# Score matmuls of 64 rows each, squares split for a ones product, more transposes at the start, an earlier merge

## What is computed

```python
u = rmsnorm(h, norm_g[0])
proj = u @ w_in                       # conv parts h, b, c; q, k, v; gates
y_conv = (bc * conv3(cc * hc)) @ w_conv_out
# 4 heads, two maps of 64 channels each, values of 128 channels
s1 = q1 @ k1.T * scale + bias ; s2 = q2 @ k2.T * scale + bias    # bias: -slope * |i - j|
a = softmax(s1) - lam * softmax(s2)
o = rmsnorm(a @ v, subln_g) * (1 - lam_init)
y_attn = o @ w_attn_out
merged = g0 * y_conv + g1 * y_attn    # g: sigmoid(gates + b_gate)
h = h + rmsnorm(merged @ w_o, norm_g[1])
f = square(relu(rmsnorm(h, norm_g[2]) @ w_ff1)) @ w_ff2
out = h + rmsnorm(f, norm_g[3])
```

## Time and profile before

| | us |
|---|---|
| median of 3 runs | 1381.34 (1381.21 to 1382.28) |
| profiled execution | 1382.01 |
| its span | 1380.3 |
| PE busy | 1370.0 (99%) |
| DVE busy | 987.8 (72%) |
| ACT busy | 601.4 (44%) |
| PE without work before the first projection | 1.4, 1.0, 0.8 and 1.0 |

### The profile page before, as it was taken

How to read it: one execution, slowest core, us unless ns; L and a number is a source line. 1 busy time by engine, 2 the same in 40 slices (tenths; PEclk the granted TensorE clock), 3 DMA queues, 4 the chain that set the end, 5 groups by cost and what they waited for, 6 DMA issues and landing times.

```text
span 1380.3 us, 17201 instructions
## 1 busy us (share of the span) xinstructions
PE 1370.0 (99%) x6233; PEld 1119.4 (81%) x6233; DVE 987.8 (72%) x1423; ACT 601.4 (44%) x931; POOL 109.6 (8%) x73
## 2 busy tenths in 40 slices
PE   8999999999999999999999999999999999999998
PEld 7778777778778888888888888888888888888886
DVE  7787796886888754576466887767664787665676
ACT  7544544544543544511243453333333444444453
POOL 0000000000000000000000233333333100000000
PEclk9999999999999999999999999999999999999999
DMA  5111111101101343454721254534445973335343
GB/s 188 46 31 31 31 32 30 45 16 30 46 15 46 108 127 109 135 163 155 270 78 61 88 178 161 167 135 157 158 143 200 364 274 112 99 118 195 112 130 109
DMA packets 141645, 162.02 MB, mean 117 GB/s; under 512 B 6861, under 2 KB 88970, under 8 KB 141450
## 3 DMA queue, kind: packets, MB, share of 16 engines
q1 hardware_dynamic: 135568, 148.27, 33.2%
q10 hardware_dynamic: 6010, 12.88, 2.4%
HBM read 114.98 MB, written 46.14 MB: 117 GB/s over the span
## 4 chain that ended last, share of the span: by engine, by line
PE 97%; DVE 2%; issue 0%; DMA 0%; ACT 0%; DVEq 0%; SPq 0%; ACTq 0%
PE psum L883 37%; PE psum L1004 28%; PE psum L1158 22%; PE psum L1135 3%; PE psum L925 3%; PE psum L970 2%; PE psum L974 1%; PE psum L1107 1%; PE psum L988 0%; DMA xn<-in_x 0%; PE psum L904 0%; DVE z L1829 0%; DVE v L2318 0%; PE psum L913 0%; DVE y L2333 0%
## 5 line engine op out<-in xcount | busy, mean ns | idle before, releaser
L1158 PE MATMUL psum<-op 128*128 128x512 f32 x1344 | 305.1, 389 | 0.1
L1158 PEld LDWEIGHTS psum<-op 128*128 128x128 f32 x1344 | 252.2, 188 | 52.8 <-issue 0.5
L883 PE MATMUL psum<-act_hi,w_hi 128*128 128x512 f32 x448 | 181.9, 406 | 1.0 <-DVE act_lo L1711 1.0
L883 PE MATMUL psum<-act_hi,w_lo 128*128 128x512 f32 x448 | 175.2, 391 | 0.0
L883 PE MATMUL psum<-act_lo,w_hi 128*128 128x512 f32 x448 | 174.5, 390 | 0.0
L2197 DVE TENSOR_TENSOR op<-v,op 128x512 fp32r<-128x512 f32 x112 | 78.6, 701 | 89.3 <-ACT op L1572 89.3
L1572 ACT ACTIVATE op<-v 128x512 fp32r<-128x512 f32 x112 | 70.7, 632 | 151.7 <-PE psum L1158 148.6
L883 PEld LDWEIGHTS psum<-act_hi,w_hi 128*128 128x128 f32 x448 | 84.2, 188 | 21.1 <-issue 4.5
L883 PEld LDWEIGHTS psum<-act_lo,w_hi 128*128 128x128 f32 x448 | 84.3, 188 | 18.0 <-issue 1.9
L883 PEld LDWEIGHTS psum<-act_hi,w_lo 128*128 128x128 f32 x448 | 84.1, 188 | 18.1
L1813 DVE CUSTOM_DVE_ANT_0 e<-psum,alibi 128x1024 f32<-128x1024 f32 x64 | 78.1, 1220 | 6.1 <-issue 5.2
(11 more groups left out here) (267 smaller groups left out, 2803.1 us busy)
## 6 DMA issues: line engine op xcount, KB each, us to landing
f_raw<-f_scratch SPq DMA_DIRECT2D x112, 256.0 KB, 2.7
w_raw<-in_w_in SPq DMA_DIRECT2D x34, 512.0 KB, 4.5
w_raw<-in_w_ff SPq DMA_DIRECT2D x32, 512.0 KB, 5.0
f_scratch<-f_out SPq DMA_DIRECT2D x56, 256.0 KB, 2.4
v<-in_w_ff SPq DMA_DIRECT2D x12, 1024.0 KB, 7.3
gates_scratch<-staging ACTq DMA_DIRECT2D x32, 256.0 KB, 2.0
gate_in<-gates_scratch SPq DMA_DIRECT2D x16, 512.0 KB, 4.2
f_scratch<-staging SPq DMA_DIRECT2D x30, 256.0 KB, 2.1
```

The lines of the kernel that those rows point to most:

```text
L883: mm = nc.tensor.matmul(bank, stat(a, kt), moving(b, kt), start=(n == 0), stop=(n == len(terms) - 1))
L1158: mm = nc.tensor.matmul(psum[:, (X_BANK, Z_BANK)[m % 2][t]], op[n % SLOTS][:, 2 + a, token_cols(t)], op[n % SLOTS][:, b], start=(m in (0, ...
```

## The change

- Score blocks: q and k are no longer stacked. Each is one tile of high parts and one of low parts, both maps one above the other in the 128 rows. For each half of the keys a block runs three passes, and each pass two matmuls of 64 rows, map 0 and map 1. ACT and DVE handle q and k in one instruction of 128 rows per unit.
- `O0` and `O1`: ACT copies the squares as a high part, DVE makes the low part in a new step `L0` or `L1`, and PE runs two `F32R` matmuls with `ones`. PE now waits for the low part. `L0` stands behind `C7` on DVE, `L1` behind `AV1`.
- Start: 34 transposes of the identity before the parameter rows and 6 behind them, instead of 24 and none.
- Gates: for the first gate pair ACT makes one copy out of PSUM earlier; the merge on DVE waits for a tanh two places earlier in their order.

```diff
-DVE_TURN = steps("C7 q0 N0 N1 N2 N3 E0 k0 T7 q1 w0 AV1 k1 w1 N4 ...
+DVE_TURN = steps("C7 L0 q0 N0 N1 N2 N3 E0 k0 T7 q1 w0 AV1 L1 k1 w1 N4 ...
-FROM_LAST_HEAD = steps("C7 O0 N0 N1 N2 N3 E0 T7 AV1 O1 N4 N5 N6 N7 E1")
+FROM_LAST_HEAD = steps("C7 L0 L1 O0 N0 N1 N2 N3 E0 T7 AV1 O1 N4 N5 N6 N7 E1")
-WARM = 24
+WARM = (34, 6)
-        ones = sb("ones", [P, P])
+        ones = sb("ones", [P, P], F32R)
...
+            use_clock(WARM[0])
             pe.wait_ge(par_landed, 16 * 4)
             pe.wait_ge(setup, 3)
             nc.tensor.transpose(psum[:, 7, 0:NPAR], par_rows[:], ident[0:NPAR, 0:NPAR]).then_inc(par_t, 1)
+            use_clock(WARM[1])
...
-                        for c in range(2):
-                            for half in range(NH):
-                                nc.tensor.matmul(psum[:, SB + 2 * c + half], q_st[c][:, n * P:(n + 1) * P],
-                                                 k_st[c][:, half_cols[half]], start=True, stop=False)
                         for half in range(NH):
-                            for c in range(2):
-                                mm = nc.tensor.matmul(psum[:, SB + 2 * c + half], q_st[c][own[c], n * P:(n + 1) * P],
-                                                      k_lo[own[c], half_cols[half]], start=False, stop=True)
+                            for a, b in PASSES:
+                                for c in range(2):
+                                    mm = nc.tensor.matmul(psum[:, SB + 2 * c + half], q_hl[a][own[c], n * P:(n + 1) * P],
+                                                          k_hl[b][own[c], half_cols[half]], start=((a, b) == PASSES[0]),
+                                                          stop=((a, b) == PASSES[-1]))
                         mm.then_inc(s_done, 1)
...
-                        pe.wait_ge(osq_ready, i * 2 + (n - 1))
+                        pe.wait_ge(osq_lo, i * 2 + (n - 1))
                         pe.wait_ge(tb_free, tb_use(i, kind, n))
-                        nc.tensor.matmul(psum[:, TBK], ones[:], dev[:], start=True, stop=True).then_inc(tb_done, 1)
+                        for a in range(2):
+                            mm = nc.tensor.matmul(psum[:, TBK], ones[:], o_sq[n][:, a], start=(a == 0), stop=(a == 1))
+                        mm.then_inc(tb_done, 1)
...
-                            for c in range(2):
-                                for rows in (own[c], other[c]):
-                                    ins = nc.scalar.activation(k_st[c][rows, half_cols[h]], psum[own[c], 1], ACT.Copy)
-                            ins.then_inc(qk_hi, 1)
+                            nc.scalar.activation(k_hl[0][:, half_cols[h]], psum[:, 1], ACT.Copy).then_inc(qk_hi, 1)
...
                         nc.scalar.activation(dev[:], psum[:, TBK], ACT.Square).then_inc(osq_ready, 1)
+                        act.wait_ge(osq_ready, i * 4 - 2 * n + 1)
+                        nc.scalar.activation(o_sq[n][:, 0], dev[:], ACT.Copy).then_inc(osq_ready, 1)
...
                 if p == GATE.first:
                     t_hi_part(GATE, 4)
+                    x_copy(GATE, 2, p)
                 g_part_hi("W11", p + 1)
...
-                if p == GATE.first:
-                    x_copy(GATE, 2, p)
...
+                    elif kind == "L":
+                        dve.wait_ge(osq_ready, i * 4 + 2 * n - 2)
+                        vec.tensor_tensor(o_sq[n][:, 1], dev[:], o_sq[n][:, 0].bitcast(F32), ALU.subtract
+                                          ).then_inc(osq_lo, 1)
...
-            last_turn("C7")
+            last_turn("C7 L0")
...
-            dve.wait_ge(gate_ready, len(GATE_ORDER))
+            dve.wait_ge(gate_ready, GATE_AT[2 * (GATE.end - 1), 0])
```

More of the change, by code:

```diff
@@ L80 @@
                  "T5 X6 M6 b1 T6 X7 M7")
-DVE_TURN = steps("C7 q0 N0 N1 N2 N3 E0 k0 T7 q1 w0 AV1 k1 w1 N4 N5 X0 M0 N6 N7 C0 E1 X1 M1 T0 C1 w2 X2 M2 T1 C2 w3 X3 M3 T2 "
+DVE_TURN = steps("C7 L0 q0 N0 N1 N2 N3 E0 k0 T7 q1 w0 AV1 L1 k1 w1 N4 N5 X0 M0 N6 N7 C0 E1 X1 M1 T0 C1 w2 X2 M2 T1 C2 w3 X3 M3 T2 "
                  "C3 c0 X4 T3 M4 VT0 C4 c1 K0 AV0 X5 w4 M5 T4 C5 b0 X6 M6 T5 C6 X7 b1 w5 M7 T6")
 V_TURN = len([x for x in ACT_TURN[:ACT_TURN.index(("VT", 0))] if x[0] == "T" and x[1] < 7])
-FROM_LAST_HEAD = steps("C7 O0 N0 N1 N2 N3 E0 T7 AV1 O1 N4 N5 N6 N7 E1")
+FROM_LAST_HEAD = steps("C7 L0 L1 O0 N0 N1 N2 N3 E0 T7 AV1 O1 N4 N5 N6 N7 E1")
 TB_ORDER = steps("O0 T7 AV1 O1 T0 T1 T2 T3 VT0 AV0 T4 T5 T6")
@@ L331, in build @@
                 at_hl = [sb(f"at_{a}", [P, TT, HALF], F32R, loop_scope) for a in ("hi", "lo")]
+                with ExitStack() as s1:
+                    o_sq = [None, sb("o_squares1", [P, 2, HALF], F32R, s1)]
                 v_hl = [sb(f"v_{a}", [P, TT, P], F32R, loop_scope) for a in ("hi", "lo")]
@@ L334, in build @@
                 inner = sb("inner", [P, S + 2], scope=loop_scope)
-                q_st = [sb(f"q_stack{c}", [P, S], F32R, loop_scope) for c in range(2)]
-                k_st = [sb(f"k_stack{c}", [P, S], F32R, loop_scope) for c in range(2)]
-                k_lo = sb("k_lo", [P, S], F32R, loop_scope)
+                q_hl = [sb(f"q_{a}", [P, S], F32R, loop_scope) for a in ("hi", "lo")]
+                o_sq[0] = sb("o_squares0", [P, 2, HALF], F32R, loop_scope)
+                k_hl = [sb(f"k_{a}", [P, S], F32R, loop_scope) for a in ("hi", "lo")]
                 with ExitStack() as s1:
@@ L479, in build @@
         zlo_ready = sem("z_lo_ready")
-        osq_ready = sem("o_squares_ready")
+        osq_ready, osq_lo = sem("o_squares_ready"), sem("o_squares_lo_ready")
         orstd_ready = sem("o_inverses_ready")
@@ L540, in build @@
         own = [slice(c * HD, (c + 1) * HD) for c in range(2)]
-        other = [own[1], own[0]]
         half_cols = [slice(h * HALF, (h + 1) * HALF) for h in range(NH)]
@@ L842, in _ @@
                                     pattern=[[-1, P]], channel_multiplier=1).then_inc(setup, 1)
-            nc.gpsimd.memset(ones[:], 1.0).then_inc(setup, 1)
+            nc.gpsimd.memset(ones[:].bitcast(F32), 1.0).then_inc(setup, 1)
             nc.gpsimd.iota(table[:], [[-1, 2 * S - P]], base=S - P, channel_multiplier=1,
@@ L889, in _, with use_clock @@
             pe.wait_ge(setup, 2)
-            for _ in range(WARM):
-                nc.tensor.transpose(psum[:, 6, 0:P], ident[:], ident[:])
+            def use_clock(count):
+                for _ in range(count):
+                    nc.tensor.transpose(psum[:, 6, 0:P], ident[:], ident[:])
+            use_clock(WARM[0])
             pe.wait_ge(par_landed, 16 * 4)
@@ L1261, in walk @@
                         if kind == "q":
-                            for c in range(2):
-                                ins = nc.scalar.activation(q_st[c][own[c], half_cols[h]], psum[own[c], 0], ACT.Copy)
-                            ins.then_inc(qk_hi, 1)
+                            nc.scalar.activation(q_hl[0][:, half_cols[h]], psum[:, 0], ACT.Copy).then_inc(qk_hi, 1)
                         elif kind == "k":
-                            for c in range(2):
-                                for rows in (own[c], other[c]):
-                                    ins = nc.scalar.activation(k_st[c][rows, half_cols[h]], psum[own[c], 1], ACT.Copy)
-                            ins.then_inc(qk_hi, 1)
+                            nc.scalar.activation(k_hl[0][:, half_cols[h]], psum[:, 1], ACT.Copy).then_inc(qk_hi, 1)
                         elif kind == "v":
@@ L1779, in walk @@
                             dve.wait_ge(qk_hi, i * 4 + (2 * h + "qk".index(kind) + 1))
[L1780 to L1784, removed]
+                            hi, lo = (q_hl, k_hl)["qk".index(kind)]
+                            vec.tensor_tensor(lo[:, cols], psum[:, "qk".index(kind)], hi[:, cols].bitcast(F32), ALU.subtract
+                                              ).then_inc(qk_ready, 1)
                         elif kind == "c":
@@ L1979, in _ @@
                 t_sum(GATE, 3, k)
-            last_turn("AV1")
+            last_turn("AV1 L1")
             for k in range(2):
```

2 lines of the change are left out of this document (1 added, 1 removed).

## The result

The changed kernel takes 1392.78 us in the median of four runs (1390.76 to 1396.70), the kernel before 1381.32 (1381.21 to 1382.28). The ratio is 1.0085, with a 95% interval of 1.0061 to 1.0108: slower by 11.5 us. Forecast were 1392.5 us and a range of 1387.2 to 1397.5.

A forecast was written before the change was run, and what follows sets the result against it. PE, busy 1370.0 of 1380.3 us, was taken to bound the kernel. Terms -3.3 + 12.2 - 0.9 + 3.2 = +11.2 us gave 1392.5 us against the median of 1381.34, range 1387.2 to 1397.5.

The forecast's parts named there:

- wait for the low part: PE at `O0` waits for `L0`, queued behind `C7` on DVE, in four places of 2.9 to 3.1 us: +12.2 us.
- ones product: `O0` and `O1` on PE: two `F32R` matmuls replace one float32 product, 0.41 us less, eight times: -3.3 us.
- score blocks: PE's score blocks: six pairs of 64-row matmuls at 0.227 us each take 1.78 us, as before: no change.
- start: Kernel start: more transposes keep the clock at 1.00, first projection moves from 14.59 to 13.73: -0.9 us.
- gates and merge: Gates and DVE's merge: PE has no wait there, and the moved copy and earlier merge change nothing: 0.
- clock behind a stall: PE's clock falls to 0.50 behind two of the four `O0` stalls, 1.6 us each: +3.2 us.
- rival 1: The stalls at `O0` come but the clock never falls: 1389.3 us, chance 0.22.
- What DVE and ACT save on q and k: Fewer copies on ACT and subtractions on DVE per head; PE waits for neither, so worth nothing.
- the pairs' load (3): In the score blocks, pairs in a row keep 0.34 us: 14.6 us more, 1404 to 1407 us, chance 0.07.
- `L0` in time (4): At `O0`, `L0` is done before PE arrives, so no stall: 1377.1 us, faster than before, chance 0.06.

The follow-up runs named there:

- early_l0: The changed kernel with `L0` moved from behind `C7` to between `C6` and `X7` of the same head on DVE: 1378.31 us, ratio 0.9977.
- plain_ones: early_l0 with the ones product again one plain float32 matmul of the squares; copy, subtraction and wait stay: 1381.46 us, ratio 0.9998.
- short_stall: The changed kernel with `L0` one DVE instruction earlier, inside `C7` ahead of its last step: 1385.66 us, ratio 1.0030.
- filled: The changed kernel with 26 identity transposes on PE ahead of each `O0`, the wait for the low part behind them: 1390.68 us, ratio 1.0066.
- early_old_merge: early_l0 with the merge's old wait for the last tanh: 1378.98 us, ratio 0.9981.
- only_blocks: The kernel before with the changed score blocks alone, including the new q and k copies and subtractions: 1382.38 us, ratio 1.0008.
- blocks_new_merge: only_blocks with the merge's new, earlier wait added: 1382.49 us, ratio 1.0003.
- long_stall: The changed kernel with `L0` one DVE instruction later in heads 1 to 3, behind `q0`'s subtraction: 1401.45 us, ratio 1.0147.

## Why the prediction was right, step by step

| step | forecast | found |
|---|---|---|
| wait for the low part | +12.2 | +12.4 in the profile |
| ones product | -3.3 | -3.3 in the profile (8 x 0.41), -3.15 in the medians (early_l0 less plain_ones) |
| score blocks | 0 | +0.1 in the profiles, and -0.3 for the pause in the first head |
| start | -0.9 | -1.0 in the profile, -0.4 in the medians |
| gates and merge | 0 | +1.0 in the profile |
| clock behind a stall | +3.2 | 0 in the profile, +2.1 in the median |
| sum | +11.2 | +8.7 in the profile, +11.5 in the medians |

The profile's terms add up to 8.9, against 8.7 between the spans (1389.0 less 1380.3). From there to the medians it is 0.7 for the profiled execution of the kernel before, which was that much above its median, and 2.1 for the clock.

The wait's figure comes from the four gaps, 12.85 us, less four units of 0.23, with 0.11 each for the unhidden load: 12.4. It is the step that decides, and it was mis-sized by 0.2. That it is this wait, and not the rest of the change, is shown by early_l0, and that it ends with `L0` by short_stall, which is 1.28 us shorter at each of the four places and took 5.0 us off the filled version's 1390.68.

The mechanism was right. That the number lies within 0.3 us of the measured one is luck: three steps were off and made up for each other, the gates by 1.0 us upwards, the clock by 1.1 downwards, and the start by 0.5 upwards in the median.

The gates' part was put at 0, by the sentence that after a stall PE is later against DVE than before, so nothing else comes late. This failed. `T7` and `AV1` behind the last head tie DVE to PE again: `AV1`'s copy is 8.12 us later than in the kernel before (442.51, now 450.63). From there DVE has all its old work and `L1`, 0.67 us, while PE has lost 0.41 to the shorter `O1`. The cover of PE's fourth X term was 0.65 us (copy done at 478.9, matmul at 479.55 in the kernel before), and it is now a gap of 1.20 between matmuls, 1.0 more than a unit. In early_l0 these two account for the whole wait: 0.67 + 0.41 - 0.65 = 0.43, and PE waits 0.43. In the changed kernel DVE loses a further 0.38, in a wait of 0.49 us ahead of its subtraction at 462.54, and PE waits 0.81. What this wait of DVE is for, and why early_l0 has none there, is open.

The clock's step had the right mechanism (filled) and too high a size: I took two falls at 1.6 us; the median has 2.1 us, and a fall costs 1.1 to 1.5 us, if the four runs had none, one, two and four, as their mean clocks suggest. In rival 1 the clock never falls: that was the profiled execution, 1390.76 against 1389.3 forecast, the gates being 1.0 of the difference. With four runs that spread over 6 us, the median's own place is partly chance.

The merge was called worth nothing. It is worth nothing in the profile that was read, where the chain through the store ended 0.3 us ahead of PE, and some 0.7 us in the median where PE comes 3 us sooner (early_old_merge). What DVE and ACT save on q and k was called worth nothing too; it is worth the 0.3 us of the pause in the first head.

Of the rivals, the pairs' load (3) is refuted by the pairs at 0.23 us. With it falls, for these pairs, the rule of the Trainium skill's page "TensorE: Matmul & The Clock Gate" (Part 3, what overlaps and what doesn't), by which a load on the same rows would wait. The rows had spoken against it already: the 1344 matmuls of 128 rows start 0.227 us apart, each with a weight load of its own, 0.19 us long, on the same 128 rows. `L0` in time (4) can be had only by moving it.

The next step for this kernel is early_l0, 3.4 us faster than before by the medians of its group.

## What to carry to other kernels

When a cheap step is put between two engines, look up when its queue comes to it, not how long it takes: 0.7 us of subtraction cost 12.4 us in one place of the queue and nothing in another, 10 us ahead of it. Here stalls of 2.9 us also let PE's clock fall in some runs, so they cost more than their length and made runs differ by up to 5.9 us; with 26 idle transposes in each, the runs lay within 0.2 us and the price was the length alone. A cover of 0.3 or 0.65 us in one profile was not enough once 0.7 us of work came in on one side, or a store took 1.6 us longer. And before medians of a few runs are compared at the level of 1 us, the runs should be sorted by their clock: only_blocks and blocks_new_merge have nearly the same median, while their runs at the upper clock are 1 us apart.

## What was not expected of the hardware

The same stall of 2.9 us, with PE busy for 0.6 of 3.5 us around it, left the clock at 1.00 at all four places of the profiled execution, while the other three runs lost 1.1 to 5.9 us. In the profile of long_stall the clock fell behind a stall of 2.76 us and not behind one of 3.44, and two of its runs had more low clock than four stretches of 3.4 us account for. About half of the executions of the kernel before (34 of 76) are at a mean clock of 0.998 or below, and are longer by 0.5 to 0.8 us on average than the others on their chip: a median of few runs moves by that. And beside a GpSimd subtraction of 128 x 512, which lasted 3.3 us, one DVE sum took its usual 2.28 us and the next 3.25.
